# Column-grouped 32-column products for the sums of squares of four heads, with the roots spread through memory

## The chip, the cores and the metric

The kernel runs on one core of one Trainium2 chip. The metric is the device time of one execution in microseconds. The kernel before takes 1570.8 us, the median of three runs (1570.33 to 1571.21).

## The reference

What must be computed is two blocks of two layers each, one after the other. In each layer of the first block (T = 272 tokens, 16 of them meta tokens) a mixer runs a gated delta rule with 4 heads beside a sparse attention with 4 heads, and a gated MLP follows. In the second block (256 tokens) the first layer has an attention mixer with 8 heads of 64, the second a retention mixer with 4 heads of 512, each followed by an MLP. Six normalisations of heads matter here. Each of them sums squares over a head's dimension and multiplies by the inverse root:

```python
def l2_norm(x):          # queries and keys of the delta rule
    return xf * lax.rsqrt(jnp.sum(xf * xf, axis=-1, keepdims=True) + EPS)
q = l2_norm(q.reshape(Bsz, T, A_HEADS, A_DK)) * (A_DK ** -0.5)
k = l2_norm(k.reshape(Bsz, T, A_HEADS, A_DK))
...
o = rms_norm(o, norm_g) * jax.nn.silu(z...)            # output of the delta rule
q = apply_rope(rms_norm(q.reshape(Bsz, T, B_HEADS, B_DH), q_norm), cos_a, sin_a)
...
q = rms_norm_2(heads(q), q_gain)                       # second block, even layer
var = jnp.mean(jnp.square(o - mu), axis=-1, keepdims=True)
o = (o - mu) * lax.rsqrt(var + EPS) * gn_gain          # second block, odd layer
```

## The kernel before

Channels lie on the 128 partitions, tokens in the free dimension. Every weight product is three products: each weight panel of 256 columns is loaded by SyncE into `stage` (two transfers of 512 KB for a slot, line 522), split by ScalarE into a high part `wH` (line 530) and by VectorE into a low part `wL` (line 539), and TensorE then adds `wH` times the high part of the input (line 552), `wH` times its low part (line 555) and `wL` times the high part (line 560). There are two slots, so a panel is loaded and split while the other is multiplied, and the two low halves come last for a slot. These products fill the four PSUM banks `lin`. Everything small (sums of squares, transposes, the delta rule, attention) uses four other banks, `aux`. The list `JOBS` (and `JOBS2`) names the small jobs in the order in which TensorE does them and gives them to the four banks in turn. `begin(name)` on TensorE waits until the bank's last job was read, `filled(name)` tells that it is written, `emptied(name)` that it is read; `full` and `read` are the waits on those. Each engine's order is written out by hand.

A sum of squares over a head is a product of an all-ones 128x128 matrix with the squares (line 895), so that the sum stands in all 128 partitions; ScalarE takes the logarithm of the bank (Ln, with `root_log`, line 1525) and then the exponential of minus half of it (Exp, `root`, line 1529), and VectorE multiplies the heads by the root. Six groups matter:

- `ssq` and `ssk`: four queries and four keys of the delta rule, from `sqh`, at 75 to 80 us; roots `rnq`, `rnk`, used at lines 2100 and 2102. Between them TensorE transposes `iab`; behind them it waits for ScalarE's squares `sq_ik`.
- `sbq`: the four attention queries, from `sq_att` (a fifth product, `sbk`, is the key's), at 123 us; roots `rnb`, used at line 2261.
- `so`: the delta rule's output, from `sqo`, at 194 us; roots `rno`, used at line 2378. Behind the squares TensorE does one gate panel and then the branch panels, whose inputs are the multiplied heads, `oH` (ScalarE, line 1704) and `oL` (VectorE, line 2381). The first two of a branch slot's four groups of products don't use these, the last two do, and wait for `oL`.
- `eq`, in the even layer: eight tiles `sqe` (two heads of 64 in each) as four products of 512 columns with the matrix `half`, at 910 us; roots `rne`, used at line 2656.
- `ow`, in the odd layer: four products of 256 columns from `sq16`, at 1296 us; roots `rn4`, used at line 2771.

The first four are done in both layers of the first block (the second layer 441 us later). GpSimd does the rope's cosine products and a few sums (line 847), and issues transfers of constants on its own queue.

## Time and profile before

| | |
|---|---|
| median of three runs | 1570.8 us |
| the profiled execution: span on the core | 1571.2 us |
| TensorE busy with products | 1558.9 us, 99% |
| VectorE, ScalarE, GpSimd busy | 1155.8, 885.8 and 53.2 us |
| chain that ended last | PE 84%, DVE 9%, ACT 3%, issue 2%, DMA 2% |

The span is from the first to the last instruction of the profiled execution; the three runs, timed without the profiler, lie within 0.9 us around the median, and the span is 0.4 us above it. Busy times overlap, so they don't add up. A row of a timeline gives a start, a busy time from the first to the last of the group, the engine, the line, the tiles written and read, the count, and in brackets how long the engine had been idle and what ended that. PEld is TensorE's loading of the stationary operand, which runs beside its products. A product of f32 operands leaves two records on each. "128\*128" is the loaded matrix, rows by columns.

### The profile page before, as it was taken

What the parts mean: (1) busy time and instruction counts of PE and PEld (TensorE: products, weight loads), DVE (VectorE), ACT (ScalarE), POOL (GpSimd) and SP (SyncE); (2) the same over time, 40 slices, a digit from 0 to 9 for tenths busy, and PEclk for the clock granted to TensorE, in tenths of its full rate; (3) what the DMA queues carried; (4) which work ended last, traced back from release to release, by engine and by line L of the source; (5) the groups of instructions that cost most, each with busy time, mean ns of one, the idle gap of its engine ahead of it and who ended that gap; (6) DMA issues with size and microseconds to landing.
All of it is one profiled execution on the core that took longest, in us unless ns stands there. A gap on an engine that the chain in (4) does not pass through costs nothing.

```text
span 1571.2 us, 34539 instructions
## 1 busy us (share of the span) xinstructions
PE 1558.9 (99%) x12620; PEld 1527.2 (97%) x12620; DVE 1155.8 (74%) x1911; ACT 885.8 (56%) x1388; POOL 53.2 (3%) x44
## 2 busy tenths in 40 slices
PE   8999999999999999999999999999999999999999
PEld 8999899999999998999999999999999999999999
DVE  7789787766568798787765768888756757678864
ACT  5665656555455755665554565666545456566652
POOL 0101001000000010010000000000010000100000
PEclk9999999999999999999999999999999999999999
DMA  6753154655546442447666546466565545656663
GB/s 216 228 154 112 55 188 148 193 175 174 175 148 187 147 120 82 151 147 239 195 185 188 173 130 188 148 201 187 181 188 182 167 140 161 187 158 191 187 192 130
DMA packets 274350, 262.98 MB, mean 167 GB/s; under 512 B 20337, under 2 KB 272785, under 8 KB 274257
## 3 DMA queue, kind: packets, MB, share of 16 engines
q1 hardware_dynamic: 272960, 257.67, 53.0%
q0 software_dynamic: 1008, 3.97, 0.8%
q8 instruction: 63, 1.03, 0.3%
q14 instruction: 31, 0.25, 0.0%
q10 hardware_dynamic: 288, 0.07, 0.0%
HBM read 256.91 MB, written 3.43 MB: 166 GB/s over the span
## 4 chain that ended last, share of the span: by engine, by line
PE 84%; DVE 9%; ACT 3%; issue 2%; DMA 2%; SPq 0%; DVEq 0%; ACTq 0%
PE lin L552 23%; PE lin L555 23%; PE lin L560 23%; PE aux L895 6%; PE lin L895 3%; DVE wL L539 3%; PE lin L606 2%; DMA stage<-in_w_in 1%; PE lin L577 1%; PE lin L641 1%; DVE cT L2045 1%; DVE nT L2501 1%; ACT wH L530 1%; DVE nL L2506 1%; PE aux L555 1%
## 5 line engine op out<-in xcount | busy, mean ns | idle before, releaser
L530 ACT ACTIVATE wH<-stage 128x1024 fp32r<-128x1024 f32 x488 | 494.2, 1049 | 461.4 <-PE lin L555 321.2
L539 DVE TENSOR_TENSOR wL<-stage,wH 128x1024 fp32r<-128x1024 f32 x488 | 571.1, 1213 | 129.9 <-PE lin L560 69.0
L552 PE MATMUL lin<-nH,wH 128*128 128x256 f32 (+2 forms) x2256 | 558.2, 286 | 0.6 <-DVE u L2550 0.3
L555 PE MATMUL lin<-nL,wH 128*128 128x256 f32 (+2 forms) x2256 | 553.5, 284 | 0.0
L552 PEld LDWEIGHTS lin<-nH,wH 128*128 128x128 f32 x2256 | 424.6, 188 | 4.0 <-issue 2.4
L555 PEld LDWEIGHTS lin<-nL,wH 128*128 128x128 f32 x2256 | 425.9, 189 | 0.9 <-issue 0.7
L560 PE MATMUL lin<-nH,wL 128*128 128x256 f32 (+2 forms) x2256 | 295.0, 283 | 0.0
L560 PEld LDWEIGHTS lin<-nH,wL 128*128 128x128 f32 x2256 | 281.4, 188 | 0.1
L552 PE MATMUL lin<-aH,wH 128*128 128x256 f32 (+1 forms) x704 | 172.3, 284 | 0.0
L555 PE MATMUL lin<-aL,wH 128*128 128x256 f32 (+1 forms) x704 | 172.2, 284 | 0.0
L555 PEld LDWEIGHTS lin<-aL,wH 128*128 128x128 f32 x704 | 132.9, 189 | 0.0
L552 PEld LDWEIGHTS lin<-aH,wH 128*128 128x128 f32 x704 | 132.9, 189 | 0.0
L560 PE MATMUL lin<-aH,wL 128*128 128x256 f32 (+1 forms) x704 | 93.1, 284 | 0.0
L560 PEld LDWEIGHTS lin<-aH,wL 128*128 128x128 f32 x704 | 88.4, 189 | 0.0
L2545 DVE SCALAR_TENSOR_TENSOR u<-lin,par,u 128x255 f32<-128x255 f32 x80 | 35.8, 480 | 35.7 <-ACT u L1813 35.3
L2444 DVE SCALAR_TENSOR_TENSOR u<-lin,parL,u 128x271 f32<-128x271 f32 (+1 forms) x40 | 17.8, 488 | 50.4 <-ACT u L1732 50.4
L2516 DVE TENSOR_TENSOR hT<-hT,lin 128x256 f32 (+1 forms) x32 | 12.1, 418 | 37.8 <-PE lin L560 37.7
L895 PE MATMUL lin<-wH,nH 128*128 128x256 f32 x160 | 38.1, 280 | 0.0
L895 PE MATMUL lin<-wH,nL 128*128 128x256 f32 x160 | 38.0, 279 | 0.0
L2550 DVE SCALAR_TENSOR_TENSOR u<-lin,par,u 128x254 f32<-128x254 f32 x80 | 34.5, 473 | 0.0
L1813 ACT ACTIVATE u<-lin,par 128x256 f32<-128x256 f32 x80 | 33.3, 467 | 0.0
L555 PE MATMUL lin<-xL,wH 128*128 128x256 f32 (+1 forms) x128 | 31.4, 285 | 0.0
(392 smaller groups left out, 2092.0 us busy)
## 6 DMA issues: line engine op xcount, KB each, us to landing
stage<-in_w_up SPq DMA_DIRECT2D x88, 512.0 KB, 4.6
stage<-in_ffn_w_up SPq DMA_DIRECT2D x88, 512.0 KB, 4.3
stage<-in_w_in SPq DMA_DIRECT2D x52, 512.0 KB, 5.0
stage<-in_w_down SPq DMA_DIRECT2D x40, 512.0 KB, 3.7
stage<-in_ffn_w_down SPq DMA_DIRECT2D x40, 512.0 KB, 4.2
stage<-in_w_gate SPq DMA_DIRECT2D x32, 512.0 KB, 4.6
stage<-in_even_w_in SPq DMA_DIRECT2D x24, 512.0 KB, 4.5
stage<-in_w_out SPq DMA_DIRECT2D x16, 512.0 KB, 4.4
```

Source lines behind the costliest of these rows:

```text
L530: nc.scalar.activation(wH[:, s, ks, 0:n], stage[:, s, ks, 0:n], ACT.Copy).then_inc(sem["whi"], 1)
L539: nc.vector.tensor_tensor(wL[:, s, ks, 0:n], stage[:, s, ks, 0:n], wH[:, s, ks, 0:n].bitcast(F32), ALU.subtract).then_inc(sem["wlo"], 1)
L552: mm = nc.tensor.matmul(banks[b][0:rows_, 0:width], wH[:, s, k, cols], xh, start=start and n == 0, stop=False)
L555: mm = nc.tensor.matmul(banks[b][0:rows_, 0:width], wH[:, s, k, cols], xl, start=False, stop=False)
L560: mm = nc.tensor.matmul(banks[b][0:rows_, 0:width], wL[:, s, k, cols], xh, start=False, stop=stop and n == len(ks) - 1)
L577: t = nc.tensor.matmul(lin[b][:, 0:width], w[:, 0, k, cols], term[x], start=first and k == 0, stop=last and k == DC - 1)
L606: t = nc.tensor.matmul(lin[b][:, 0:width], w[:, 0, k, cols], term[x], start=first and k == 0, stop=last and k == DC - 1)
L895: return nc.tensor.matmul(o_, l_, r_, start=start, stop=stop)
L1813: f(u2[:, 2 * s + c, :], xg2[:, 2 * s + c, :] if first else lin[2 * s + c][:, 0:SEQ], Copy, scale=par[:, DEPTH + j, ds(t2 + s * FC + 2 * i ...
L2444: own.done(v.scalar_tensor_tensor(acc, x, w, acc, ALU.mult, ALU.add))
L2545: own.done(v.scalar_tensor_tensor(u2[:, q, 1:SEQ], (xg2[:, q, :] if first else lin[q])[:, 0:SEQ - 1], w, u2[:, q, 1:SEQ], ALU.mult, ALU.add))
L2550: v.scalar_tensor_tensor(u2[:, q, 2:SEQ], (xg2[:, q, :] if first else lin[q])[:, 0:SEQ - 2], w, u2[:, q, 2:SEQ], ALU.mult, ALU.add).then_i ...
```

## The change

In each of the six groups the four products now load only 32 columns of the ones (or `half`) and write to partitions 0, 32, 64 and 96 of one bank. ScalarE takes one Ln and one Exp of that bank and issues a transfer of four partitions, one of each head (for `eq` two transfers of four), to a small array in memory. GpSimd waits for this transfer and issues another, `spread`, that fetches the rows back into all partitions of `rnq`, `rnk`, `rnb`, `rno`, `rne` or `rn4` (544 KB, for `rne` twice 512 KB, for `rn4` 512 KB). VectorE waits for that one. `sbk` stays as it is. The odd layer's TensorE now waits once for both halves of the squares.

```diff
-    ["ms1"] + [f"ssq{h}" for h in range(4)] + ["ta"] + [f"ssk{h}" for h in range(4)] + ["sik", "gc", "tv"]
+    ["ms1", "ssq", "ta", "ssk", "sik", "gc", "tv"]
...
-    + [f"sbq{h}" for h in range(4)] + ["sbk"] + ["Y1_4", "Y2_4"] + [x for b in range(3) for x in (f"kt{b}", f"vt{b}")]
+    + ["sbq", "sbk"] + ["Y1_4", "Y2_4"] + [x for b in range(3) for x in (f"kt{b}", f"vt{b}")]
...
-    + [f"so{h}" for h in range(4)] + [("loop", 2, [f"br{b}" for b in range(4)])] + ["ms2"]
+    + ["so"] + [("loop", 2, [f"br{b}" for b in range(4)])] + ["ms2"]
...
+        rows_q, rows_k, rows_b, rows_o = (nc.dram_tensor(f"rows_{x}", (4, T), F32) for x in "qkbo")
+        rows_e = nc.dram_tensor("rows_e", (8, 512), F32)
+        rows_w = nc.dram_tensor("rows_w", (4, SEQ), F32)
...
+            def spread(to, rows_, stored, landed):
+
+                pool.wait_ge(*stored)
+                pool.dma_start(to.rearrange("p h t -> p (h t)"), bass.AP(rows_, 0, [[0, P], [1, to.shape[1] * to.shape[2]]])).then_inc(sem[landed], 16)
...
+                    if n == 1:
+                        spread(rnq[:, :, :], rows_q, (sem["stored_q"], at("stored_q", l, 16)), "roots_q")
+                        spread(rnk[:, :, :], rows_k, (sem["stored_k"], at("stored_k", l, 16)), "roots_k")
+                    if n == 2:
+                        spread(rnb[:, 0:4, :], rows_b, (sem["stored_b"], at("stored_b", l, 16)), "roots_b")
...
+                spread(rno[:, :, :], rows_o, (sem["stored_o"], at("stored_o", l, 16)), "roots_o")
...
+            pool.wait_ge(sem["erows_out"], 32)
+            for n in range(2):
+                pool.dma_start(rne[n * HALF:(n + 1) * HALF, :, :].rearrange("p c t -> p (c t)"), bass.AP(rows_e, 2048 * n, [[0, HALF], [1, 2048]])).then_inc(sem["eroots_in"], 16)
...
+            spread(rn4[:, :, :], rows_w, (sem["orows_out"], 16), "oroots_in")
...
-                def head_squares(h0):
-                    for h in range(h0, h0 + 4):
-                        name = f"ss{'qk'[h // 4]}{h % 4}"
-                        mm(begin(name, l)[:, 0:T], ones, sqh[:, h, :]).then_inc(filled(name), 1)
+                def head_squares(name, x):
+
+                    ps = begin(name, l)
+                    for h in range(4):
+                        t = mm(ps[32 * h:32 * h + 32, 0:T], ones[:, 0:32], x[:, h, :])
+                    t.then_inc(filled(name), 1)
...
-                head_squares(0)
+                head_squares("ssq", sqh[:, 0:4])
                 turned("ta", iab, IDX_DIM, 16, (sem["iab"], at("iab", l, 1)))
-                head_squares(4)
+                head_squares("ssk", sqh[:, 4:8])
...
-                for h, name in enumerate([f"sbq{h}" for h in range(4)] + ["sbk"]):
-                    mm(begin(name, l)[:, 0:T], ones, sq_att[:, h, :]).then_inc(filled(name), 1)
+                head_squares("sbq", sq_att[:, 0:4])
+                mm(begin("sbk", l)[:, 0:T], ones, sq_att[:, 4, :]).then_inc(filled("sbk"), 1)
...
-                for h in range(4):
-                    mm(begin(f"so{h}", l)[:, 0:T], ones, sqo[:, h, :]).then_inc(filled(f"so{h}"), 1)
+                head_squares("so", sqo)
...
+            ps = begin("eq", L)
             for c in range(4):
-                mm(begin(f"eq{c}", L)[:, :], const("half", P), sqe[:, 2 * c:2 * c + 2, :].rearrange("p c t -> p (c t)")).then_inc(filled(f"eq{c}"), 1)
+                t = mm(ps[32 * c:32 * c + 32, :], const("half", P)[:, HALF - 16:HALF + 16], sqe[:, 2 * c:2 * c + 2, :].rearrange("p c t -> p (c t)"))
+            t.then_inc(filled("eq"), 1)
...
+            pe.wait_ge(sem["osum"], 2)
+            ps = begin("ow", L)
             for h in range(4):
-                pe.wait_ge(sem["osum"], h // 2 + 1)
-                mm(begin(f"ow{h}", L)[:, 0:SEQ], ones, sq16[:, 4 * h, :]).then_inc(filled(f"ow{h}"), 1)
+                t = mm(ps[32 * h:32 * h + 32, 0:SEQ], ones[:, 0:32], sq16[:, 4 * h, :])
+            t.then_inc(filled("ow"), 1)
...
-                def root(last, to, bias_):
+                def root(last, to, bias_, counter="rn"):
                     act.wait_ge(*read(last, l))
-                    f(to[:, :, :], to[:, :, :], Exp, scale=-0.5, bias=bias_).then_inc(sem["rn"], 1)
+                    f(to, to, Exp, scale=-0.5, bias=bias_).then_inc(sem[counter], 1)
+
+                def rows_stored(to, x, n, counter):
+                    act.wait_ge(sem["roots"], at("roots", l, n))
+                    act.dma_start(bass.AP(to, 0, [[T, 4], [1, T]]), x[0:P:32, :]).then_inc(sem[counter], 16)
...
-                root_log([f"ssq{h}" for h in range(4)], rnq, 1.0)
+                root_log(["ssq"], root_q[:, :].unsqueeze(1), 1.0)
+                root("ssq", root_q[:, :], lnq_col, "roots")
+                rows_stored(rows_q, root_q, 1, "stored_q")
...
-                root_log(["ssk0"], rnk, 1.0)
+                root_log(["ssk"], root_k[:, :].unsqueeze(1), 1.0)
+                root("ssk", root_k[:, :], 0.0, "roots")
+                rows_stored(rows_k, root_k, 2, "stored_k")
...
-                root_log([f"sbq{h}" for h in range(4)] + ["sbk"], rnb, 1.0 / P)
-                root("sbk", rnb, 0.0)
+                root_log(["sbq"], root_late[:, :].unsqueeze(1), 1.0 / P)
+                root("sbq", root_late[:, :], 0.0, "roots")
+                rows_stored(rows_b, root_late, 3, "stored_b")
+                root_log(["sbk"], rnb, 1.0 / P, 4)
+                root("sbk", rnb[:, 4, :], 0.0)
...
+                root_log(["so"], root_late[:, :].unsqueeze(1), 1.0 / P)
+                root("so", root_late[:, :], 0.0, "roots")
+                rows_stored(rows_o, root_late, 4, "stored_o")
...
+            act.wait_ge(*full("eq", L))
+            f(roots_e, bank("eq")[:, :], Ln, bias=eps_col, scale=1.0 / 64).then_inc(emptied("eq"), 1)
+            act.wait_ge(*read("eq", L))
+            f(roots_e, roots_e, Exp, scale=-0.5).then_inc(sem["eroots"], 1)
+            act.wait_ge(sem["eroots"], 1)
             for n in range(2):
-                act.wait_ge(*read(f"eq{2 * n}", L))
-                act.wait_ge(*read(f"eq{2 * n + 1}", L))
-                f(rne[:, 4 * n:4 * n + 4, :], rne[:, 4 * n:4 * n + 4, :], Exp, scale=-0.5).then_inc(sem["ern"], 1)
+                act.dma_start(bass.AP(rows_e, 2048 * n, [[512, 4], [1, 512]]), roots_e[16 * n:P:32, :]).then_inc(sem["erows_out"], 16)
...
+            act.wait_ge(*full("ow", L))
+            f(roots_w, bank("ow")[:, 0:SEQ], Ln, bias=eps_col, scale=1.0 / 512).then_inc(emptied("ow"), 1)
+            act.wait_ge(*read("ow", L))
+            f(roots_w, roots_w, Exp, scale=-0.5).then_inc(sem["oroots"], 1)
+            act.wait_ge(sem["oroots"], 1)
+            act.dma_start(bass.AP(rows_w, 0, [[SEQ, 4], [1, SEQ]]), roots_w[0:P:32, :]).then_inc(sem["orows_out"], 16)
...
-                dve.wait_ge(sem["rn"], at("rn", l, 1))
+                dve.wait_ge(sem["roots_q"], at("roots_q", l, 16))
                 v.tensor_tensor(cT[:, 0:4, :], cT[:, 0:4, :], rnq[:, :, :], ALU.mult).then_inc(sem["qk_unit"], 1)
-                dve.wait_ge(sem["rn"], at("rn", l, 2))
+                dve.wait_ge(sem["roots_k"], at("roots_k", l, 16))
                 v.tensor_tensor(cT[:, 4:8, :], cT[:, 4:8, :], rnk[:, :, :], ALU.mult).then_inc(sem["qk_unit"], 1)
...
+                dve.wait_ge(sem["roots_b"], at("roots_b", l, 16))
                 v.scalar_tensor_tensor(rawT[:, 16:20, :], rawT[:, 16:20, :], pc(K_QN), rnb[:, 0:4, :], ALU.mult, ALU.mult).then_inc(sem["att_unit"], 1)
...
+                dve.wait_ge(sem["roots_o"], at("roots_o", l, 16))
                 for h in range(4):
-                    dve.wait_ge(sem["rno"], at("rno", l, h + 1))
                     v.tensor_tensor(zT[:, h, :], zT[:, h, :], rno[:, h, :], ALU.mult).then_inc(sem["oa"], 1)
...
-                dve.wait_ge(sem["ern"], n + 1)
+                dve.wait_ge(sem["eroots_in"], 32)
                 v.scalar_tensor_tensor(x, x, p2(0, gain), rne[:, 4 * n:4 * n + 4, :], ALU.mult, ALU.mult).then_inc(sem["eunit"], 1)
...
-                dve.wait_ge(sem["ovar"], h + 1)
+                dve.wait_ge(sem["oroots_in"], 16)
```

ScalarE's order around the queries' and keys' squares in the first layer, from the first Ln to the last of these squares' Ln (and now to the copy of `ikr`) (`root_q`, `root_k` are the tiles of four heads in one; `rows_q`, `rows_k` lie in memory). Before:

```order
L1525 ACTIVATE rnq<-aux,c_55 128x272 [waits aux_full1]
L1525 ACTIVATE rnq<-aux,c_55 128x272 [waits aux_full2]
L1525 ACTIVATE rnq<-aux,c_55 128x272 [waits aux_full3]
L1525 ACTIVATE rnq<-aux,c_55 128x272 [waits aux_full0]
L1537 ACTIVATE ab<-aux 16x16 [waits aux_full1]
L1538 ACTIVATE ab<-aux 128x32
L1525 ACTIVATE rnk<-aux,c_55 128x272 [waits aux_full2]
L1543 ACTIVATE sq_ik<-lin 64x272 x2
L1546 ACTIVATE ikr<-lin 64x272 x2
L1550 ACTIVATE gl<-gm 128x12 [waits sp_in]
L1552 ACTIVATE gl<-gl,c_55 128x12 [waits act_own]
L1525 ACTIVATE rnk<-aux,c_55 128x272 [waits aux_full3]
```

And now:

```order
L1554 ACTIVATE root_q<-aux,c_55 128x272 [waits aux_full1]
L1558 ACTIVATE root_q<-root_q,c_55 128x272 [waits aux_read1]
L1562 DMA rows_q<-root_q 4x272 [waits roots]
L1572 ACTIVATE ab<-aux 16x16 [waits aux_full2]
L1573 ACTIVATE ab<-aux 128x32
L1554 ACTIVATE root_k<-aux,c_55 128x272 [waits aux_full3]
L1558 ACTIVATE root_k<-root_k 128x272 [waits aux_read3]
L1562 DMA rows_k<-root_k 4x272 [waits roots]
L1580 ACTIVATE sq_ik<-lin 64x272 x2
L1583 ACTIVATE ikr<-lin 64x272 x2
```

Eight Ln went for two; the two Exp of 1088 columns, which stood behind the rows shown, went for two of 272 columns right behind their Ln, each with a transfer. The whole of the keys' root now stands ahead of `sq_ik`, where before one Ln of it stood.

ScalarE's order at the squares `so`, ahead of the gate and branch panels' splits. Before:

```order
L1674 ACTIVATE oH<-aux 128x4x128 [waits aux_full1]
L1698 ACTIVATE rno<-aux,c_55 128x272 [waits aux_full3]
L1698 ACTIVATE rno<-aux,c_55 128x272 [waits aux_full0]
L1698 ACTIVATE rno<-aux,c_55 128x272 [waits aux_full1]
L1698 ACTIVATE rno<-aux,c_55 128x272 [waits aux_full2]
L1701 ACTIVATE rno<-rno 128x272 [waits aux_read3]
L1701 ACTIVATE rno<-rno 128x272 [waits aux_read0]
L1701 ACTIVATE rno<-rno 128x272 [waits aux_read1]
L1701 ACTIVATE rno<-rno 128x272 [waits aux_read2]
L1704 ACTIVATE oH<-zT 128x272 [waits oa] x4
L530 ACTIVATE wH<-stage 128x1024 [waits panel_in2,whi_used]
```

And now (`root_late` is the tile of the four heads):

```order
L1711 ACTIVATE oH<-aux 128x4x128 [waits aux_full0]
L1554 ACTIVATE root_late<-aux,c_55 128x272 [waits aux_full2]
L1558 ACTIVATE root_late<-root_late 128x272 [waits aux_read2]
L1562 DMA rows_o<-root_late 4x272 [waits roots]
L1738 ACTIVATE oH<-zT 128x272 [waits oa] x4
L539 ACTIVATE wH<-stage 128x1024 [waits panel_in2,whi_used]
```

Four Ln and four Exp became one of each and a transfer, and the copies `oH` stand right behind it; the wait of these for VectorE's products `zT` is as before, but VectorE's first of these now waits for `roots_o`, the landing of GpSimd's transfer.

GpSimd's order in a layer, from the first cosine product to the sums of squares behind the mixer, now (before it held the same rows without the four transfers):

```order
L890 TENSOR_TENSOR rawT<-rawT,c_55 128x4x256 [waits swapped]
L865 DMA rnq<-rows_q 128x1088 [waits stored_q]
L865 DMA rnk<-rows_k 128x1088 [waits stored_k]
L890 TENSOR_TENSOR ikr<-ikr,c_55 128x272 [waits swapped]
L865 DMA rnb<-rows_b 128x1088 [waits stored_b]
L890 TENSOR_TENSOR bkr<-bkr,c_55 128x272 [waits rope_sin]
L890 TENSOR_TENSOR rawT<-rawT,c_55 128x1088 [waits rope_sin]
L865 DMA rno<-rows_o 128x1088 [waits stored_o]
L856 TENSOR_TENSOR sq_106<-sq_106 128x544 [waits sq]
```

The transfers stand between the cosine products in the program's order, each with a wait for ScalarE's transfer; the first cosine product is ahead of all of them.

## Rows read from the trace of the kernel before

**Rows 1.** The page, busy time of the engines.

```profile
PE 1558.9 (99%) x12620; PEld 1527.2 (97%) x12620; DVE 1155.8 (74%) x1911; ACT 885.8 (56%) x1388; POOL 53.2 (3%) x44
```

**Rows 2.** Timeline of PE at two groups of squares: start us, us, engine, line.

```profile
75.50 2.00 PE L895 MATMUL aux<-sqh,c 128*128 128x272 f32 x8
...
909.59 3.59 PE L895 MATMUL aux<-sqe,c 128*128 128x512 f32 x8
```

**Rows 3.** Timeline of weight loads: products in one, then in two, column groups.

```profile
190.45 0.30 PEld L895 LDWEIGHTS aux<-cT,S 128*128 128x128 f32 x2
190.67 0.30 PEld L895 LDWEIGHTS aux<-QD,vn 128*128 128x128 f32 x2
...
955.09 1.78 PEld L895 LDWEIGHTS aux<-PTe,vtk 128*64 128x64 f32 x32 [0.29 <-issue]
```

**Rows 4.** Timeline of 75 to 90 us, at the squares of queries and keys.

```profile
77.25 1.62 ACT L1525 ACTIVATE rnq<-aux,c 128x272 f32<-128x272 f32 x4
...
80.14 0.30 PEld L895 LDWEIGHTS aux<-sq_ik,c 128*128 128x128 f32 x2 [0.31 <-ACT sq_ik L1543]
...
84.97 0.43 ACT L1529 ACTIVATE rni<-rni 128x272 f32<-128x272 f32 x1
...
88.72 1.28 DVE L2100 TENSOR_TENSOR cT<-cT,rnq 128x1088 f32<-128x1088 f32 x1
```

**Rows 5.** Timeline of ACT at its only DMA issues, at the start.

```profile
0.75 0.42 ACTq L1423 DMA_DIRECT2D gain<-in_first_gain  x1
```

**Rows 6.** DMA issues: xcount, KB each, median us from issue to landing.

```profile
stage<-in_w_branch_a SPq DMA_DIRECT2D x8, 512.0 KB, 3.7
stage<-in_w_branch_b SPq DMA_DIRECT2D x8, 512.0 KB, 4.8
...
c<-in_c POOLq DMA_DIRECT2D x2, 528.0 KB, 3.9
...
za<-zero POOLq DMA_DIRECT2D x2, 256.0 KB, 6.1
...
ik_s<-ikr SPq DMA_DIRECT2D x8, 34.0 KB, 1.8
```

**Rows 7.** Timeline of 194 to 209 us, from the squares `so` to the branch products.

```profile
194.31 0.91 ACT L1698 ACTIVATE rno<-aux,c 128x272 f32<-128x272 f32 x2
...
195.19 1.18 PE L895 MATMUL aux<-sqo,c 128*128 128x272 f32 x4 [0.49 <-DVE oL L2323]
...
197.32 1.50 DVE L2378 TENSOR_TENSOR zT<-zT,rno 128x272 f32<-128x272 f32 x4
198.74 1.49 DVE L2381 TENSOR_TENSOR oL<-zT,oH 128x272 fp32r<-128x272 f32 x4
...
202.44 0.91 DVE L2111 TENSOR_SCALAR rawT<-lin,parL 128x272 f32<-128x272 f32 x2 [2.21 <-PE lin L560]
203.27 4.62 DVE L539 TENSOR_TENSOR wL<-stage,wH 128x1024 fp32r<-128x1024 f32 x4
...
206.27 2.16 PE L560 MATMUL lin<-oH,wL 128*128 128x272 f32 x16
```

**Rows 8.** Timeline of DVE, 914 to 927 us, even mixer.

```profile
914.89 2.48 DVE L2656 SCALAR_TENSOR_TENSOR raw<-raw,par,rne 128x1024 f32<-128x1024 f32 x2 [2.74 <-ACT rne L1855]
...
924.58 0.76 DVE L2644 TENSOR_TENSOR ght<-lin,ght 128x256 f32<-128x256 f32 x2 [3.32 <-PE lin L560]
925.74 1.29 DVE L2607 TENSOR_TENSOR Pe<-aux,c 128x512 f32<-128x512 f32 x2 [0.40 <-PE aux L895]
```

**Rows 9.** Timeline of 1300 to 1316 us, odd mixer.

```profile
1300.89 3.25 DVE L2771 SCALAR_TENSOR_TENSOR oR<-oR,par,rn 128x256 f32<-128x256 f32 x8 [1.40 <-ACT rn L1937]
1304.25 2.36 DVE L539 TENSOR_TENSOR wL<-stage,wH 128x1024 fp32r<-128x1024 f32 x2
...
1313.41 2.05 PE L560 MATMUL lin<-nH,wL 128*128 128x256 f32 x16
```

**Rows 10.** Timeline of DVE at the roots `rnb`, first layer.

```profile
130.59 1.35 DVE L2261 SCALAR_TENSOR_TENSOR rawT<-rawT,parL,rnb 128x1088 f32<-128x1088 f32 x1
```

More of the change, by code:

```diff
@@ L201 @@
 JOBS2 = (
-    ["ems"] + [f"eq{c}" for c in range(4)] + ["e00", "e01"] + [f"e1{e}" for e in range(4)] + [f"et0{g}" for g in range(2)]
+    ["ems", "eq", "e00", "e01"] + [f"e1{e}" for e in range(4)] + [f"et0{g}" for g in range(2)]
     + [f"et1{g}{b}" for g in range(2) for b in range(2)] + ["ev0", "ev1", "emf", "oms"]
     + [f"os{h}" for h in range(4)] + [f"oo{h}{e}" for h in range(4) for e in range(2)]
-    + [f"ow{h}" for h in range(4)] + ["omf"]
+    + ["ow", "omf"]
 )
@@ L213 @@
     "sq": DC, "rstd": 2, "n": 2 * DC, "nh": DC, "nl": DC,
[L214 removed]
+    "conv": 12, "silu": 3, "sq_heads": 2, "sq_att": 1, "sq_ik": 1, "rn": 2, "roots": 4, "stored_q": 16, "stored_k": 16, "stored_b": 16, "stored_o": 16, "roots_q": 16, "roots_k": 16, "roots_b": 16, "roots_o": 16, "qk_unit": 2, "att_unit": 3,
     "sp_in": 1, "sp_ln": 1, "gt": 4, "eg": 4, "dec": 3, "kdx": 1, "qe": 1,
     "rates_out": 3 * 16, "rates_in": 3 * 16, "rates_exp": 1, "rope_cos": 4, "rope_sin": 4, "swapped": 2 * 4 * 16, "rope": 4, "score": 6, "ml": 2 * len(UPPER), "mt_out": 3 * 16, "mt_in": 3 * 16, "solved": 1, "bt_out": 2 * 16, "b_out": 3 * 16, "x_back": 2 * 16, "a_back": 3 * 16,
[L217 removed]
+    "nmx": 3, "soft": 2, "pn": 3, "ob_h": 3, "sqo": 3, "oa": 4, "oa_h": 4, "oa_l": 4,
     "gates": 12, "y": 8, "yh": 4, "yl": 4,
@@ L1552, in layer @@
                 f(gl[:, :, :], gl[:, :, :], Ln, bias=one_col).then_inc(sem["sp_ln"], 1)
-                root_log([f"ssk{h}" for h in range(1, 4)], rnk, 1.0, 1)
                 root_log(["sik"], rni, 1.0 / P)
-                root("ssq3", rnq, lnq_col)
-                root("ssk3", rnk, 0.0)
-                root("sik", rni, 0.0)
+                root("sik", rni[:, :, :], 0.0)
                 split_hi(act, m0 + 6, 0)
@@ L1695, in layer @@
                 weighted_values(2)
-                for h in range(4):
-                    act.wait_ge(*full(f"so{h}", l))
-                    f(rno[:, h, :], bank(f"so{h}")[:, 0:T], Ln, bias=eps_col, scale=1.0 / P).then_inc(emptied(f"so{h}"), 1)
-                for h in range(4):
-                    act.wait_ge(*read(f"so{h}", l))
-                    f(rno[:, h, :], rno[:, h, :], Exp, scale=-0.5).then_inc(sem["rno"], 1)
+                root_log(["so"], root_late[:, :].unsqueeze(1), 1.0 / P)
+                root("so", root_late[:, :], 0.0, "roots")
+                rows_stored(rows_o, root_late, 4, "stored_o")
                 for h in range(4):
@@ L1931, in _ @@
             act.preload_act_table_set(EXP_LN)
-            for h in range(4):
-                act.wait_ge(*full(f"ow{h}", L))
-                f(rn4[:, h, :], bank(f"ow{h}")[:, 0:SEQ], Ln, bias=eps_col, scale=1.0 / 512).then_inc(emptied(f"ow{h}"), 1)
-            for h in range(4):
-                act.wait_ge(*read(f"ow{h}", L))
-                f(rn4[:, h, :], rn4[:, h, :], Exp, scale=-0.5).then_inc(sem["ovar"], 1)
+            act.wait_ge(*full("ow", L))
[4 more added lines that the diff above has]
+            act.dma_start(bass.AP(rows_w, 0, [[SEQ, 4], [1, SEQ]]), roots_w[0:P:32, :]).then_inc(sem["orows_out"], 16)
             act.preload_act_table_set(SILU)
```

19 lines of the change are left out of this document (10 added, 9 removed).

## The prediction

> **What bounds the kernel now.** I read the page's busy times first: TensorE has products 99% of the span [rows 1], so the time is the length of TensorE's work plus some 12 us of waits, and an edit counts only by what it does to TensorE's stream: columns taken out of it, or a wait put into it. VectorE has a quarter of the span free on average, but a panel's last third (line 560) needs the `wL` that VectorE made, so VectorE becomes the bound where it is held up longer than its lead. I therefore went through the timeline at each of the six groups and noted for each what TensorE needs next, from whom, and how early it is there.
>
> **What TensorE saves.** A group of four products of 272 columns is busy 2.00 us, the four of 512 columns 3.59 [rows 2]. The kernel has no 32-column products. It has serial ones and 64-column ones that alternate between two column halves of the array: serial, two 128-column records start 0.22 us apart for the pair, 0.11 each; of the alternating ones 32 take 1.78 us, 0.056 each [rows 3]. So two column groups run side by side, at half the price per record. From serial 0.11 a record of 272 columns costs 0.11 x 272/128 = 0.234, four products (eight records) 1.87, of 512 columns 3.5, of 256 columns 1.76. With four groups side by side a quarter remains: 0.47, 0.88 and 0.44. Saved: 1.40 for each of the eight groups of 272 (four in each of two layers) = 11.2; 2.64 for `eq`; 1.32 for `ow`; together **15.2 us**, if everything behind were ready. The bounds of the price are no overlap at all (nothing saved) and a quarter; I take the quarter, since the halving shows in the nearest rows.
>
> **What the roots cost instead.** Before, a root was in all partitions as soon as Exp had run. Now it goes Ln, Exp, ScalarE's store, GpSimd's fetch. A small store of 34 KB landed 1.8 us after its issue, a fetch of 528 KB on GpSimd's queue, nearly the same as 544 KB, took 3.9; that is 5.7 alone. Of two 512 KB transfers that SyncE issues one behind the other for a branch slot, the second takes 1.1 longer than the first, 4.8 for 3.7 [rows 6]; a fetch that shares the memory with them I take at 1 us more, so the **trip takes 5.7 to 6.7 us**. The far upper bound for a GpSimd transfer is the 256 KB one at 6.1 [rows 6]: 2.2 more than 3.9.
>
> The Trainium skill ("DMA: Bandwidth & Descriptors", Anatomy of one DMA) gives GpSimd's transfers 2.0 us plus bytes/436e3; an estimate from it for 544 KB is 3.3 us. The row says 3.9 for 528 KB, and I go by the row; by the page each trip would be 0.6 shorter and the sum below about 1.8 us lower.
>
> **`ssq`, `ssk`.** TensorE waits behind these groups for ScalarE's `sq_ik`, already 0.31 us before [rows 4]. So the end of this stretch is ScalarE's. From the first Ln at 77.25 on, ScalarE did four Ln in 1.62 and one more of 0.49 (two take 0.91 at 0.42 apart [rows 7]) ahead of `sq_ik`. Now it does Ln, Exp and an issue twice: an Exp of 272 columns is 0.43 [rows 4], an issue of a transfer on ScalarE 0.42 [rows 5], so 2 x (0.49 + 0.43 + 0.42) = 2.68, against 2.11: 0.57 more, and four dependent steps with 0.1 each between them, about 1.0. TensorE's 2.8 us saved turn into a wait, and it loses 1.0 more here. In the second layer TensorE comes to this place later relative to ScalarE; I take 0.4. The q root is stored about 80 and in all partitions by 84.5, the k root about 1.7 later, 86 to 88. Needed at 88.7 or, since ScalarE is spared two long Exp, a microsecond earlier [rows 4]: hidden by VectorE's split ahead of it. Without that cover each microsecond late would go to TensorE by way of line 2136.
>
> **`sbq`.** It saves 1.40 a layer, but TensorE's next transposes share their banks with what VectorE evicts behind the index scores, which are VectorE's own chain. So this group's saving only pays back the loss of the one above in the first layer, and meets a transfer in the second. Its root: Ln and Exp come at about 124.3, store 125.3 to 127.2, fetch to about 131.2, against a need at 130.6 [rows 10]. That is 0.6 late for the `wL` behind it, which has about that much lead. Together with `ssq`, `ssk` I put 0 for the first layer and 0 for the second, each with bounds from -1.2 (saved) to +1.5.
>
> **`so`.** Here the path is short. First Ln at 194.31, Exp behind it, store issued about 195.3, landed 197.1, fetch 3.9 + 1 because the branch panels are being loaded just then: R = 202.0 for the root in `rno`. Before, `zT` started at 197.32. What is queued behind the wait on VectorE: `zT` (the next row starts 1.42 later), `oL` 1.49, the gate's `rawT` (0.83 to the next), then the low parts of the branch slot, half of 4.62 [rows 7]. R + 1.42 + 1.49 + 0.83 + 2.31 = R + 6.05, and TensorE's line 560 on this slot can't start earlier; it started at 206.27 [rows 7]. With R = 202.0: 208.05, **1.8 us later** than before, although TensorE is there 1.40 + 0.49 earlier (the wait of 0.49 for the bank of `oL` goes too, since `so` takes one bank that is free). ScalarE's copies and its split for the second slot end about R + 3.9, and are needed 8 us behind R. The same in the second layer: 3.6. The point where this turns is R = 200.2: then it is zero, and at R = 198.4 or less both layers together save 3.8.
>
> **`eq`.** The group ends about 2.6 us earlier, 910.6 for 913; then Ln 0.7, Exp 0.7, two issues, landed about 914.8; two fetches of 512 KB side by side on GpSimd's queue, 3.9 and about 1.5 for the second: A = 920, with 919 to 921.5. Before, VectorE multiplied at 914.89. Behind it are a multiplication 2.48, a `wL` 2.36 (its length in [rows 9]), and `ght` 0.76; then `Pe`, which started at 925.74 [rows 8]. A + 5.6 = 925.6. So VectorE comes to the scores when it came before, and TensorE's four last score products wait for it to free banks. The 2.64 saved are all spent: 0, with bounds of -1.2 and +1.5.
>
> **`ow`.** TensorE waits for both sums now, so only some 0.2 is saved. Roots: the table load ends at about 1299, Ln, Exp, issue at 1299.9, landed 1301.7, fetch to 1306. VectorE starts 5 us late (1300.89 before) but its `wL`, 1304.25 to 1306.6, is wanted only at 1313.41 [rows 9], 6.8 later: hidden, and later `wL` have 5.8 us. Where the trip took 1 us longer it would begin to cost.
>
> **Sum.** 3.6 (`so`) - 0.2 (`ow`) + 0 (the rest) = **+3.4 us** on the profiled 1571.2, which stands 0.4 above the median. Against the median 1570.8 that is **1574.2**.
>
> **Rivals.**
>
> *Shorter trip: faster.* What decides is R in `so`, 200.2. If the trip is 2 us shorter than I take, R = 200 and A = 918: `so` gives 0.4, `eq` 2.0, `ow` 0.2: 1568.2; with 3.6 us shorter `so` gives 3.8, `eq` 2.6: 1564.2. For it: a store of four rows is tiny and its fetch reads few addresses. Against: 3.9 is a median with little other load. Chance 0.2.
>
> *Every saving arrives.* 1570.8 - 15.2 = 1555.6. It needs other roots than by way of memory, or leads of 6 us everywhere; [rows 4] show TensorE waiting for ScalarE already. Chance 0.03.
>
> *The 32-column products don't run side by side* (that the change doesn't do what it says). Then `so` is 0.9 later a layer (1.4 less the 0.49), `eq` 2.6, `ssq` to `sbq` about 1 a layer, `ow` 1: 3.4 + 1.8 + 2.6 + 2 + 1 = +10.8, 1581.6. [rows 3] speak against it. The Trainium skill ("TensorE: Matmul & The Clock Gate", Part 3, Measured speedup) measured 2.38 times the pace with three column groups; no row here has more than two. Chance 0.07.
>
> *Longer trip.* With 2 us more (6.1 for a GpSimd transfer [rows 6]): `so` 2 x 2, `eq` 2, `sbq` 2 x 1.5, `ow` 1: +10 on 3.4, 1584. The Trainium skill ("SBUF — State Buffer", SBUF: two separate sides) tells of such a transfer of 620 ns that took 3100 when VectorE was busy in its fast modes; that would be this rival by its 2.5 us. At `so` VectorE is idle when the fetch is issued, at `eq` and `sbq` it isn't. Chance 0.2.
>
> **Numbers.** The likeliest case has 0.5, with a range of its own of 1571 to 1578. A measurement of this kernel can tell 0.2%, 3.1 us, so no change is 1567.7 to 1573.9. Faster: 0.15 of the shorter trip and 0.03, 0.18. No change: 0.05 of the shorter trip and 0.2 of the likeliest, 0.25. Slower: the other 0.3 and the last two rivals, 0.57. The range of 8 in 10 cuts the far ends: 1566 to 1583.
>
> **What the changed trace would show.** TensorE's four squares in 0.5 to 0.7 us, and in 0.9 for 512 columns; if 2 us, the third rival. A wait for `sq_ik` of 2 us or more. `zT` x `rno` starting at 202.0 less 0.2 or so, and TensorE waiting at a line 560 of the first branch slot, or at `oL` ahead of it, by 3 to 4 us. VectorE idle before line 2656's multiplication from 912 to 920. No wait of TensorE behind `ow`. My number is wrong above all if the trip isn't 6.7 us at `so`: each microsecond there is 2 us of time, and 5 or 6 with the other places.

## Result and the profile after

The changed kernel takes **1594.2 us** (median of four runs, 1592.4 to 1595.0), the kernel before 1570.6 (four runs beside it, 1569.9 to 1571.2). The ratio is **1.0143, with a 95% interval of 1.0131 to 1.0155**: slower, as forecast, but by 23.7 us where the prediction had 3.4, and outside its range. The profiled executions differ by 22.0 (span 1593.2 for 1571.2).

First the page of the changed kernel, its busy times.

```profile
PE 1558.3 (98%) x12620; PEld 1524.8 (96%) x12620; DVE 1155.7 (73%) x1911; ACT 867.2 (54%) x1350; POOL 59.3 (4%) x55
```

TensorE is still busy 98% of the span, so against [rows 1] the loss seems to be in longer work, not in waits. The waits of TensorE (us in total, times, longest) name what is new:

```profile
PE lin L561 <- DVE rawT L2145: 10.2, 2, 5.1
PE aux L919 <- ACT sq_ik L1580: 7.1, 2, 3.7
PE aux L919 <- DVE raw L2691: 3.1, 1, 3.1
```

These are `so`, `ssq`/`ssk` and `eq`: 20.4 us of waits, and the squares got much cheaper besides. Timeline of PE at the first of each kind (start, us; compare [rows 2]):

```profile
75.59 0.67 PE L919 MATMUL aux<-sqh,c 128*32 128x272 f32 x8
926.99 1.06 PE L919 MATMUL aux<-sqe,c 128*32 128x512 f32 x8
```

Four products of 272 columns in 0.67 us for 2.00, of 512 columns in 1.06 for 3.59: the four column groups do run side by side. But waits and savings don't add up to the difference. What is missing is in the granted clock. Each row below is a stretch of time, with the busy time of PE, PEld, DVE, ACT and POOL, the granted clock (PEclk, 1.00 is full speed), the DMA share and GB/s; first the changed kernel, then the kernel before:

```profile
82.20:88.00 5.80, 5.80 (x23) 5.57 (x24) 4.77 (x9) 4.06 (x8) 0.55 (x1) 0.50 0.96 325
88.00:92.00 4.00, 4.00 (x35) 3.94 (x33) 2.37 (x2) 0.38 (x2) 0.00 (x0) 1.00 0.17 63
212.00:218.00 6.00, 5.94 (x27) 5.94 (x28) 4.95 (x6) 4.87 (x5) 0.00 (x0) 0.52 0.50 153
530.00:535.00 5.00, 4.76 (x24) 4.68 (x25) 4.01 (x8) 4.19 (x9) 0.53 (x1) 0.67 0.93 273
660.00:665.00 5.00, 4.70 (x22) 4.70 (x23) 5.00 (x6) 4.04 (x4) 0.00 (x0) 0.51 0.37 108
948.00:952.00 4.00, 4.00 (x21) 4.00 (x22) 3.83 (x7) 2.45 (x8) 0.00 (x0) 0.57 0.18 64
```

```profile
82.00:88.00 6.00, 5.64 (x48) 5.53 (x47) 3.00 (x6) 5.97 (x13) 0.00 (x0) 1.00 0.55 175
605.00:610.00 5.00, 4.55 (x28) 3.94 (x27) 4.30 (x14) 3.92 (x4) 0.00 (x0) 0.54 0.01 3
```

Behind each of the new waits TensorE runs at half speed (the lower of its two levels, 1.2 GHz for 2.4) for some 3 to 6 us, and those stretches count as busy: 23 products in 5.8 us for 48 in 6. That is why the page shows a full engine. The last row is no part of the loss: the kernel before too has such a stretch, in the second layer's triangular solve, where TensorE's longest wait is 0.45 us, and the changed kernel has the same one 12 us later.

I then set each product of TensorE against the same product of the kernel before; the difference of their starts, at the named places, says where the 22 us arose:

```
place                 later by, us        of it: wait   half clock
ssq, ssk, layer 0     0    -> 4.3           2.1          2.5
so, layer 0           4.3  -> 10.4          3.5          2.6
ssq, ssk, layer 1     10.4 -> 12.5          0.9          1.3
so, layer 1           12.2 -> 17.2          3.1          1.9
eq                    17.0 -> 21.1          2.6          1.5
ow                    21.9 -> 22.1
```

The wait's column is net of the cheaper squares. `sbq` and all stretches between move it by under 1 us each. So a little over half of the loss (12.2 us) is waits, and the rest (9.8 us) is TensorE at half clock behind them.

**Where the trips stand.** The timeline at the first `so` (in the square brackets: idle time before, and what ended it):

```profile
198.04 0.67 PE L919 MATMUL aux<-sqo,c 128*32 128x272 f32 x8
199.76 0.52 ACTq L1562 DMA_DIRECT2D rows_o<-root_late  x1
200.77 0.37 SPq L531 DMA_DIRECT2D stage<-in_w_branch_a  x1
201.67 0.59 POOL L865 DMA_DIRECT2D rno<-rows_o  x1 [50.08 <-DMA rows_o<-root_late]
201.77 0.37 SPq L531 DMA_DIRECT2D stage<-in_w_branch_b  x1
208.69 1.50 DVE L2413 TENSOR_TENSOR zT<-zT,rno 128x272 f32<-128x272 f32 x4 [6.95 <-DMA rno<-rows_o]
211.51 0.90 DVE L2145 TENSOR_SCALAR rawT<-lin,parL 128x272 f32<-128x272 f32 x2
212.06 0.59 PE L561 MATMUL lin<-oH,wH 128*128 128x272 f32 x1 [5.12 <-DVE rawT L2145]
```

The store has landed by 201.67, 1.9 us after its issue, as taken from [rows 6]. The fetch, issued between two loads of branch panels, takes 7 us, where the prediction had 4.9. `zT` by the roots starts 11.4 us later than in [rows 7], 7.1 when TensorE's 4.3 at that point is taken off, for the 4.7 of the prediction. The DMA issues (KB each, median us to landing):

```profile
rnq<-rows_q POOLq DMA_DIRECT2D x2, 544.0 KB, 4.4
rnk<-rows_k POOLq DMA_DIRECT2D x2, 544.0 KB, 6.2
rno<-rows_o POOLq DMA_DIRECT2D x2, 544.0 KB, 6.7
rn<-rows_w POOLq DMA_DIRECT2D x1, 512.0 KB, 3.6
```

At `ssq`/`ssk`, ScalarE and then TensorE (compare [rows 4]):

```profile
78.60 1.06 ACTq L1562 DMA_DIRECT2D rows_q<-root_q  x1
79.71 0.17 ACT L1572 ACTIVATE ab<-aux 16x16 f32<-16x16 f32 x1 [1.14 <-issue]
80.82 0.49 ACTq L1562 DMA_DIRECT2D rows_k<-root_k  x1
81.36 0.79 ACT L1580 ACTIVATE sq_ik<-lin 64x272 f32<-64x272 f32 x2 [0.57 <-ACT root_k L1558]
82.20 0.82 PE L919 MATMUL aux<-sq_ik,c 128*128 128x272 f32 x1 [3.75 <-ACT sq_ik L1580]
```

TensorE's product of `sq_ik` comes 2.1 us later than in [rows 4]; the first store's issue alone held ScalarE 1.06 us. At `eq` the two stores and two fetches:

```profile
929.51 1.04 ACTq L1889 DMA_DIRECT2D rows_e<-sqe  x2
932.86 1.06 POOL L901 DMA_DIRECT2D rne<-rows_e  x2 [46.31 <-DMA rows_e<-sqe]
940.19 2.48 DVE L2691 SCALAR_TENSOR_TENSOR raw<-raw,par,rne 128x1024 f32<-128x1024 f32 x2 [10.73 <-DMA rne<-rows_e]
942.73 2.58 PE L919 MATMUL aux<-raw 64*128 64x128 f32 x24 [3.10 <-DVE raw L2691]
946.26 1.73 PE L919 MATMUL aux<-raw 64*128 64x256 f32 x8 [0.96 <-DVE Pe L2642]
```

TensorE waits here twice, 3.10 for `raw` and 0.96 for `Pe`, and the clock is at half only behind the second (0.57 in 948 to 952). Stores to fetch issue 3.35, fetches to use 7.3. With TensorE 17.0 later here, A is 923.2 in the time of the kernel before, for the 920 of the prediction.

### The profile page after: what moved, and what is told of

It reads as the page before. It is cut to its first block, busy times and chain, and to the rows that moved or that the text cites. A ratio compares the mean times of both kernels' runs of the same rounds, so it can differ in the third digit from the quotient of the medians.

```text
span 1593.2 us, 34511 instructions
## 1 busy us (share of the span) xinstructions
PE 1558.3 (98%) x12620; PEld 1524.8 (96%) x12620; DVE 1155.7 (73%) x1911; ACT 867.2 (54%) x1350; POOL 59.3 (4%) x55
## 4 chain that ended last, share of the span: by engine, by line
PE 77%; DVE 12%; DMA 5%; ACT 3%; issue 3%; SPq 0%; ACTq 0%; DVEq 0%; POOL 0%
PE lin L561 21%; PE lin L564 21%; PE lin L569 21%; PE aux L919 4%; PE lin L919 4%; DVE wL L548 3%; PE lin L615 2%; DMA stage<-in_w_in 1%; PE lin L586 1%; PE lin L650 1%; DVE cT L2079 1%; DMA rno<-rows_o 1%; DVE nT L2536 1%; ACT wH L539 1%; DVE nL L2541 1%
```

## Experiments

All ratios are to the kernel before, run on the same chip, with 95% intervals; its medians there were 1570.9 (for `so` as before, the filled idle time, no trip, and `sq_ik` first), 1570.8 (for the fetch by ScalarE, the loads held, `sbq` with `ow`, and the rounded squares) and 1572.2 (for the other four). The changed kernel is "after".

### `so` as before

After, with the four products, four Ln and four Exp of `so` put back:

```diff
-                head_squares("so", sqo)
+                for h in range(4):
+                    mm(begin(f"so{h}", l)[:, 0:T], ones, sqo[:, h, :]).then_inc(filled(f"so{h}"), 1)
```

> The changed kernel with one of its six groups, the squares `so` of the delta rule's output, done as before (four full products, four Ln, four Exp, no transfers), in both layers. Theory (the root's trip is late at `so`, TensorE idles 5 us, and then runs some 5 us at half clock): TensorE's lag against the kernel before grows in the changed kernel from 4.3 to 10.4 us at `so` of the first layer and from 12.2 to 17.2 in the second, 11 us together, and all of it goes: 1583. Rival (the cost is spread over all narrow products and the extra traffic): two of ten groups, so about 5 us: 1589.

Measured 1581.7, ratio 1.0066 [1.0044, 1.0087]: 12 to 13 us less than after, 6 a layer. The wait for `rawT` is gone, the one for `sq_ik` stays at 7.1 in two. `so` is the largest part of the loss, in size as the differences of the starts say (6.1 + 5.0).

### The idle time filled with products nobody reads

After, with products of `ones` by `ones` in front of each of the three waits (16, 22 and 13 of 128 columns), so that TensorE isn't idle:

```diff
+                pe.wait_ge(*read("so", l))
+                for _ in range(22):
+                    mm(bank("so")[:, 0:P], ones, ones)
```

> The changed kernel with products of the ones by themselves put where TensorE idles: 16 ahead of the wait for `sq_ik`, 22 ahead of the branch panels, 13 ahead of the even layer's scores, 128 columns each, into a bank that nobody reads then. The work that matters is the same and waits as long. Theory (the clock falls because TensorE idled): the granted clock stays at 1.00 behind these places and the 9 to 10 us of half-clock running go: 1585. Rival (the clock falls with the 32-column products, or with the traffic of the fetches): the clock still falls, 1594 or a little more.

Measured 1589.7, 1.0114 [1.0097, 1.0131]. Its stretches:

```profile
82.00:88.00 6.00, 6.00 (x46) 5.92 (x47) 5.01 (x9) 3.95 (x8) 0.55 (x1) 1.00 0.96 309
530.00:535.00 5.00, 5.00 (x42) 5.00 (x42) 4.62 (x8) 2.92 (x5) 0.00 (x0) 1.00 1.02 340
948.00:952.00 4.00, 4.00 (x36) 4.00 (x36) 3.83 (x5) 1.45 (x5) 0.00 (x0) 1.00 0.00 0
```

The clock stays at 1.00 where after had 0.50, 0.67 and 0.57, while the narrow products are all there and the fetches still run beside them (DMA share 0.96 and 1.02 in the first two stretches). So at these places the idling of TensorE brought the clock down. But of the 9.8 us of half clock only 4.5 came back, by the medians. Part of the rest is the clock again, at another place. This trace, first row, has a stretch at half clock in the first layer's triangular solve that after, second row, doesn't have:

```profile
170.00:175.00 5.00, 5.00 (x33) 4.38 (x32) 3.79 (x13) 3.41 (x7) 0.00 (x0) 0.50 0.00 0
170.00:175.00 5.00, 4.62 (x44) 4.04 (x44) 4.86 (x17) 4.93 (x7) 0.00 (x0) 1.00 0.00 0
```

It costs this execution 2.7 us. Of the 4.8 that it gains on after everywhere else, 2.1 are left at the end. Not every execution can have it: the four took 1592.9, 1590.4, 1589.0 and 1587.6 with mean granted clocks of 0.996, 0.997, 1.000 and 1.000, and the trace is of the first. For part of what is still missing, the next engine to be late shows (us in total, times, longest):

```profile
PE aux L919 <- DVE MT L2179: 2.5, 2, 1.8
```

VectorE's `MT` is late too (TensorE waits 0.4 for it in the kernel before), and the slow stretch had hidden it.

### The same filling at `so` alone

> The changed kernel with 22 products of the ones by themselves (128 columns each, 4.8 us together) ahead of the branch panels alone, where TensorE idles 5.1 us at `so` in each layer; the other idle places stay. Theory (idling of that length costs the clock, and nothing else waits behind it): TensorE waits under 1 us for the branch's late products, which come no later than before, the clock stays at 1.00 behind them, and the lag that grew by 2.6 and 1.9 us while the clock was at half goes: 1589.7. Rival (clock and idling are not linked): 1594 or more.

Measured 1593.2, 1.0132 [1.0116, 1.0147]. The stretches behind the two `so` (compare 0.52 and 0.51 above):

```profile
210.00:215.00 5.00, 4.80 (x38) 4.57 (x37) 5.00 (x9) 4.94 (x6) 0.00 (x0) 1.00 0.07 16
660.00:665.00 5.00, 4.52 (x37) 4.30 (x37) 4.81 (x8) 3.50 (x4) 0.00 (x0) 1.00 0.62 201
```

The clock is full again. The time is lower by 1.7 us by the ratios, but the intervals overlap, so a gain in the whole kernel isn't shown, and the 1589.7 of the forecast was missed. In the trace the products behind `so` in the first layer do come 2.2 us earlier. Part is lost again at `eq`: TensorE waits 4.1 for `raw` where after has 3.1.

### No trip at all

After, with the stores and fetches left out; VectorE multiplies by the root tile that ScalarE wrote:

```diff
-                v.tensor_tensor(cT[:, 0:4, :], cT[:, 0:4, :], rnq[:, :, :], ALU.mult).then_inc(sem["qk_unit"], 1)
+                v.tensor_tensor(cT[:, 0:4, :], cT[:, 0:4, :], bf(root_q[:, :], 1, [P, 4, T]), ALU.mult).then_inc(sem["qk_unit"], 1)
```

> The changed kernel without any of the stores and fetches: VectorE multiplies all four heads by the narrow root tile as it lies, so each head is multiplied by the root of a head that its partition happens to hold, and the output is another one. The narrow products, one Ln and one Exp remain. Theory (all that is lost is in the trips and the two stores on ScalarE): `so` 3.8 faster than before, `eq` 2.6, `sbq` about 1, and at `ssq`, `ssk` TensorE still waits about 1.5 us for `sq_ik`: 1564 to 1567. Rival (narrow products bring a cost of their own, such as the clock): above 1571.

Measured 1563.7, 0.9962 [0.9948, 0.9976]. This is the ceiling of the idea with these orders: 6 to 7 us with a free broadcast, not the 15.2 of the squares' own time. One reason is that even here TensorE waits for ScalarE's chain:

```profile
PE aux L909 <- ACT sq_ik L1569: 3.8, 2, 2.0
```

The trips with all that follows from them therefore cost 28 us by the ratios (0.0181 of 1571), 30 by the medians.

### `sq_ik` ahead of the roots

After, and below also the kernel without trips, with ScalarE's two squares `sq_ik` moved ahead of the first Ln:

```diff
+                for p0 in (0, IDX_DIM):
+                    t = f(sq_ik[p0:p0 + IDX_DIM, :], lin[0][0:IDX_DIM, 0:T], Square)
+                t.then_inc(sem["sq_ik"], 1)
                 root_log(["ssq"], root_q[:, :].unsqueeze(1), 1.0)
```

> The changed kernel with ScalarE's two squares `sq_ik` moved ahead of the queries' root and its store. Theory (ScalarE's two roots and two stores, 3.7 us, stand ahead of what TensorE waits for, and the idle time costs clock too): TensorE finds `sq_ik` ready; of the lag that grew by 4.3 and 2.1 us there nearly all goes, and the 2 x 2.8 us of saved columns stay: about 9 less, 1585. Rival (the next thing TensorE needs from ScalarE or VectorE, the logits' chain, is as late): the wait moves to line 990 or the products with `gtri`, and less than 3 us are won: 1591 or more.

Measured 1598.2, 1.0177 [1.0160, 1.0194]: slower than after by 4 us (by the ratios 5), where a gain was forecast. TensorE no longer waits for `sq_ik`, but it waits all the same (first line; the second is ScalarE's wait that it comes from):

```profile
PE aux L919 <- DVE MT L2170: 6.3, 2, 3.1
91.19 0.22 ACT L1603 ACTIVATE beta<-beta 68x16 f32<-68x16 f32 x1 [3.77 <-DMA beta<-logits]
```

The clock now falls behind this wait (0.66 in 100 to 105, 0.50 in 550 to 555, where after has 1.00). `beta` goes through memory, from `iab` to `logits` and back, by small transfers of SyncE, three each way. Either the fetches of the roots delay these, or the chain is that long by itself. The next kernel has no fetches:

> The kernel without stores and fetches (wrong roots, as told there) with `sq_ik` moved ahead of the queries' root as well. With the trips this move won nothing, since TensorE then waited 3.1 us for VectorE's `MT`, whose chain goes through the tiny transfers of the logits. Theory (these transfers were slow because 1 MB of fetched roots ran at the same time): without the trips the move pays, TensorE's 3.8 us at `sq_ik` go and 1 us comes back at `MT`: 1561. Rival (the chain of the logits is as late without the traffic): TensorE waits 3 us for `MT` a layer, 1564 or more.

Measured 1567.8, 0.9973 [0.9961, 0.9985], no better than without trips and `sq_ik` where it was (0.9962; the intervals overlap).

```profile
PE aux L909 <- DVE MT L2154: 6.1, 2, 3.1
89.15 0.22 ACT L1592 ACTIVATE beta<-beta 68x16 f32<-68x16 f32 x1 [3.01 <-DMA beta<-logits]
```

The wait for `MT` is nearly the same without the fetches, so they aren't what makes it. What TensorE saves in the squares it must wait again, for `sq_ik` or for `MT`. And the move isn't free by itself: ScalarE's `ab`, now behind the two squares, comes 1.0 us later than without the move (78.67 for 77.67), SyncE's first issue for `logits` 1.2 later (82.34 for 81.11), and TensorE's products with `gtri` 1.3 later (98.62 for 97.31). The fetches lengthen the chain further: from the last issue for `logits` to the first for `beta` it takes 4.1 and 6.1 us in the two layers with them, 3.6 and 3.9 without.

### Who slows the fetch at `so`

Two kernels, both from after. In the first, ScalarE issues the fetch itself behind its store:

```diff
+                act.wait_ge(sem["stored_o"], at("stored_o", l, 16))
+                act.dma_start(rno[:, :, :].rearrange("p h t -> p (h t)"), bass.AP(rows_o, 0, [[0, P], [1, 4 * T]])).then_inc(sem["roots_o"], 16)
```

> The changed kernel with the fetch of `rno` issued by ScalarE, which waits for its own store and then issues, instead of by GpSimd. ScalarE has nothing to do there until VectorE's products. Theory A (the fetch at `so` takes 6.7 us, not the 3.9 of the row before, because the two 512 KB branch transfers run at the same time): it lands as late, 1594. Theory B (GpSimd's queue is what is slow there): the fetch takes about 4.5 and TensorE's wait shrinks by 2 us a layer, with the clock some 6 us in all: 1588.

In the second, SyncE holds its loads for the second branch slot until the fetch has landed:

```diff
+                    if s:
+                        sp.wait_ge(sem["roots_o"], at("roots_o", l, 16))
```

> The changed kernel with SyncE's loads for the second slot of the first branch panel held until `rno` has landed (and the loop over branch loads written out). Theory A (shared memory time): the fetch, alone now, takes 4 to 4.5 us instead of 6.7, TensorE waits 2.5 us less a layer, and half-clock running shrinks: 1587. Theory B (GpSimd's queue): the fetch takes 6.7 still, 1594 or later.

Measured: by ScalarE 1589.4, 1.0111 [1.0096, 1.0127]; loads held 1587.4, 1.0102 [1.0087, 1.0118]. Their fetches, `zT` and the wait of TensorE, first by ScalarE, then with the loads held:

```profile
rno<-rows_o ACTq DMA_DIRECT2D x2, 544.0 KB, 5.0
205.02 1.50 DVE L2414 TENSOR_TENSOR zT<-zT,rno 128x272 f32<-128x272 f32 x4 [5.07 <-DMA rno<-rows_o]
PE lin L561 <- DVE rawT L2146: 6.3, 2, 3.2
```

```profile
rno<-rows_o POOLq DMA_DIRECT2D x2, 544.0 KB, 4.1
205.44 1.50 DVE L2417 TENSOR_TENSOR zT<-zT,rno 128x272 f32<-128x272 f32 x4 [4.18 <-DMA rno<-rows_o]
PE lin L561 <- DVE rawT L2149: 4.9, 2, 2.6
```

With no loads beside it the same fetch on the same queue takes 4.1 for 6.7, near the 3.9 of [rows 6]: the two 512 KB loads cost it 2.6. But the queue has a part too. Issued by ScalarE, with both loads beside it nearly as in after, it takes 5.0 and not 6.7. Theory A there had it land as late as before, at 1594; the measured 1589.4 is near theory B's 1588. So the fetch is slow where both come together, the loads and GpSimd's queue, and either remedy takes most of it away. Held loads gave 6.4 us back in two layers, ScalarE's issue 5.0. What differs between the queues, the runs don't show; VectorE isn't it, since it had been idle for 6.95 us when the root came.

### Each of the hidden trips

Before, with `sbq` and `ow` changed and nothing else; then `ow` alone, then `sbq` alone:

> The changed kernel with `ssq`, `ssk`, `so` and `eq` done as before; only `sbq` (both layers) and `ow` keep 32-column products and the trip through memory. Theory (only these two trips are hidden; the lag fell by some 0.5 us over `sbq` in each layer of the changed kernel and stayed level over `ow`): 1569.5, no measurable difference to the kernel before. Rival (each trip costs, hidden or not, by its traffic): three of the nine trips remain, 1573 or more.

> Only `ow` as in the changed kernel, all else as before. It shares out the 3.7 us that `sbq` and `ow` together cost. Theory (the roots of `ow` reach VectorE 6.5 us later than before, and one of its low parts is then late for TensorE): 1.5 us slower than before, 1572.3. Rival (hidden as predicted, the cost is at `sbq`): 1570.6.

> Only `sbq` as in the changed kernel, in both layers, all else as before. Theory: saved columns and the wait of 0.8 us for `rnb`, which delays VectorE's `X`, about cancel, with up to 2 us for the clock where the small waits of the triangular solve grow: 1572. Rival (the trip is hidden and the columns saved stay): 1569 or less.

Measured 1574.5, 1.0025 [1.0016, 1.0035] for both; 1573.9, 1.0009 [1.0000, 1.0018] for `ow`; 1573.3, 1.0005 [0.9996, 1.0014] for `sbq`, which can't be told from no change. `ow` is not hidden. VectorE's start and TensorE's wait further on:

```profile
1307.18 3.26 DVE L2796 SCALAR_TENSOR_TENSOR oR<-oR,par,rn 128x256 f32<-128x256 f32 x8 [8.02 <-DMA rn<-rows_w]
1319.47 2.15 PE L569 MATMUL lin<-nH,wL 128*128 128x256 f32 x16 [0.75 <-DVE wL L548]
```

VectorE is 6.3 later than in [rows 9], and the 5.8 us that later `wL` have are used up. The 1569.5 forecast for both was missed. Why both together cost 3.9 where the two apart sum to some 2.2 is for the most part the clock: each run has its mean granted clock on record, and at an equal 0.999 the pair is 2.6 slower than before (1573.4 for 1570.8), `ow` 1.5 (1572.9 for 1571.4) and `sbq` 0.8 (1572.3 for 1571.4), with two or three runs of each changed kernel. Five of the pair's eleven runs had 0.995 to 0.997 and took 1575.2 to 1579.1; none of before's was below 0.998. Whether the two changes together bring the clock down more often, or this was chance, isn't settled.

### The other way to cheaper squares

Before, with squares and ones rounded to fp32r and everything else where it was (`ow` and `sik` left in fp32). Its sums of squares are those of rounded squares.

```diff
-                        mm(begin(name, l)[:, 0:T], ones, sqh[:, h, :]).then_inc(filled(name), 1)
+                        mm(begin(name, l)[:, 0:T], onesR[:, :], sqh[:, h, :]).then_inc(filled(name), 1)
```

> The kernel before, with another way to the same end: ScalarE writes the squares `sqh`, `sq_att`, `sqo` and `sqe` rounded to fp32r, and the ones and `half` are kept in a rounded copy, so that a full 128-column product is one pass record instead of two at twice the price (about 0.13 us for 0.45 at 272 columns). No roots travel; `sik` and `ow` stay in fp32. Theory (the columns saved were real, 10.9 + 2.6 us of TensorE's time, and the trips ate them; at `ssq`, `ssk` TensorE only waits longer for `sq_ik`): about 7 less than before, as without the trips, 1564. Rival (TensorE's places behind these groups were bound by ScalarE's and VectorE's chains, which are as long as before here): 1568 to 1571.

Measured **1567.1, 0.9977 [0.9967, 0.9986]**: faster than the kernel before, by 3.6 us.

```profile
75.25 0.67 PE L897 MATMUL aux<-sqh,onesR 128*128 128x272 f32 x4
PE aux L897 <- DVE oL L2330: 2.3, 2, 1.2
PE aux L966 <- ACT rnq L1530: 2.0, 2, 1.5
```

Four products take the 0.67 us of the packed ones (four records, since a product is one pass), and the sums are in all partitions with no trip. It had 1564 as its forecast. The trace has new waits, none over 1.5 us, and the granted clock is 0.50 in 80 to 85 behind one of them; that these two keep the rest is likely but wasn't tested.

## Why the prediction was off

**TensorE saves: right as a price, wrong as a gain.** I took a quarter per record from [rows 3]; the group of 2.00 us is now busy 0.67, the tail of the last product in it, and what follows it starts 1.4 us earlier, as worked out. The Trainium skill ("TensorEngine Tiling (Array Packing)", Theoretical Speedup) gives up to four times for tiles of at most 32 rows or columns, and the trace agrees, with 3.4 times in busy time for 512 columns (3.59 to 1.06). But without trips only 6 to 7 of the 15 us arrive.

**`so`: the step that failed.** Its chain (Ln, Exp, store, fetch, `zT`, gate, branch products) was right. The place of TensorE's wait was nearly so: not the first slot's last products (line 560), but the third group ahead of them, where `oL` is wanted and the gate's `rawT` came last. One size was off. The term "fetch 3.9 + 1 because the branch panels are being loaded" measured 6.7 to 7 in all; held loads showed that the sharing is worth 2.6 on GpSimd's queue and not 1, while on ScalarE's queue the same fetch beside the same loads took 5.0, about the 4.9 of the term. And a term was missing: behind a wait of 5.1 us TensorE was at half clock for some 5 us, 2.6 and 1.9 more. Instead of +1.8 a layer it came to +6.1 and +5.0, and undoing `so` gave 12 to 13 back. The Trainium skill ("TensorE: Matmul & The Clock Gate", HAM oscillation — how this bites in real kernels) says that idle gaps can bring the clock down, and the rows of 82 to 88 and 212 to 218 agree, with 0.50 and 0.52 behind waits of 3.75 and 5.12 us. I had weighed no such thing, though the prediction itself forecast a wait of 3 to 4 us here.

**The longer trip** was a rival, at 1584 and 0.2. It is what happened at `so` and `eq`, at `so` with a cause that can be taken away (the loads beside it, or the queue); at `eq` the cause wasn't tested. It is still 10 us short, and 9.8 is what the half clock cost, which it lacked too.

**`ssq`, `ssk`: 1.0 and 0.4, put to 0 with `sbq`.** ScalarE's extra was 2.1 and not 1.0, since one issue took 1.06 for the 0.42 of [rows 5] and the hand-over to `sq_ik` 0.57 for 0.1. Behind it again half clock: +4.3 and +2.1. That `sbq` pays this back did not happen. That hardly any saving arrives here holds, and not for `sq_ik` alone: with it early and no trips, `MT` makes TensorE wait 6.1 in the two layers.

**`eq`: A = 920 was 923.2.** The stores landed at 915.9 (932.86 less 17.0) for 914.8, and the fetches took 7.3 for 5.2. VectorE was late for the first score products already (3.1 us of wait for `raw`), and again for the last ones, where the prediction had it just in time (0.96 for `Pe`): +4.1 for 0, of it 1.5 half clock.

**`sbq`: 0, right.** Its 1.0005 can't be told from no change. **`ow`: hidden, wrong** by a little: the delay was 6.3 for the 5 that I set against a slack of 5.8. The prediction had the turning point right ("where the trip took 1 us longer").

Against the sum of +3.4: `so` +7.5 more, `ssq`/`ssk` +6.4, `eq` +4.1, the rest about +0.7, with the 3.4 together 22.1. These are not independent prices. Filling the idle time gave 4.5 and not 9.8, as the clock fell elsewhere in some executions and the other engines' chains came next.
